# Up tiles with high and low tokens as one 512-column operand, in two mixture-of-neurons layers on one core

## What is computed

```python
sv, si = lax.top_k(sc, PEER_TOPK)
cand = (sv[:, :, 0, :, None] + sv[:, :, 1, None, :]).reshape(c, PEER_HEADS, -1)
best, pos = lax.top_k(cand, PEER_TOPK)
eidx = jnp.take_along_axis(cidx, pos, axis=-1)
g = jax.nn.softmax(best, axis=-1)
a = jnp.einsum('cd,chkd->chk', xc, w_up[eidx]).astype(jnp.float32)
act = (jax.nn.gelu(a, approximate=False) * g).astype(xc.dtype)
return jnp.einsum('chk,chkd->cd', act, w_down[eidx])
```

## Time and profile before

| | |
|---|---|
| median of three runs | 2362.91 us |
| profiled execution, its own time | 2365.95 us |
| its span, first to last instruction | 2363.9 us |
| mean granted TensorE clock | 0.995 |
| up stage of layer 0 | 193.9 to 611.0 us |
| up stage of layer 1 | 1115.1 to 1532.0 us |

### The profile page before, as it was taken

The page is one execution under the profiler, slowest core; times in us unless marked ns, Lnnn a source line. Parts: engine busy times, 40 slices in busy tenths (PEclk is TensorE's granted clock), DMA queues, the critical chain, the costliest instruction groups (busy, mean ns, idle before and its releaser), DMA issues.

```text
span 2363.9 us, 45061 instructions
## 1 busy us (share of the span) xinstructions
PE 2327.5 (98%) x15648; PEld 2089.7 (88%) x15648; DVE 1690.3 (72%) x3195; ACT 1326.6 (56%) x2502; POOL 42.9 (2%) x85
## 2 busy tenths in 40 slices
PE   8999999999999999999999999999999998999998
PEld 8889999999888888899999999988888886788776
DVE  5767996999655555675997799956556577767555
ACT  5655545877545544445455677754555454665454
POOL 1000000000000000000000000000000000000000
PEclk9999999999999999999999999999999999999999
DMA  7455665444566666555556544566665653246454
GB/s 241 129 170 163 183 179 178 137 142 144 179 194 191 192 194 194 163 178 174 183 179 182 157 143 143 161 195 193 208 189 178 182 172 107 72 137 195 129 157 141
DMA packets 137305, 397.44 MB, mean 168 GB/s; under 512 B 12448, under 2 KB 13776, under 8 KB 136400
## 3 DMA queue, kind: packets, MB, share of 16 engines
q1 hardware_dynamic: 134432, 384.97, 54.0%
q0 software_dynamic: 2448, 10.56, 1.3%
q10 hardware_dynamic: 288, 0.10, 0.0%
HBM read 394.54 MB, written 1.05 MB: 167 GB/s over the span
## 4 chain that ended last, share of the span: by engine, by line
PE 91%; DVE 5%; issue 2%; ACT 2%; DMA 0%; DVEq 0%; ACTq 0%; POOLq 0%; POOL 0%; SPq 0%
PE bank L998 31%; PE bank L1014 29%; PE bank L896 12%; PE bank L902 8%; PE bank L1027 4%; PE bank L955 1%; PE bank L943 1%; ACT wh L1336 1%; DVE wl L1731 1%; PE bank L928 1%; PE bank L948 1%; PE bank L979 1%; DVE aux L1769 0%; PE bank L907 0%; PE bank L1212 0%
## 5 line engine op out<-in xcount | busy, mean ns | idle before, releaser
L1731 DVE TENSOR_TENSOR wl<-raw,wh 128x1024 fp32r<-128x1024 f32 (+1 forms) x732 | 893.7, 1222 | 542.9 <-ACT wh L1336 531.7
L1336 ACT ACTIVATE wh<-raw 128x1024 fp32r<-128x1024 f32 (+1 forms) x732 | 771.8, 1055 | 643.5 <-PE bank L1014 337.3
L998 PE MATMUL bank<-xh,wh 128*128 128x256 f32 x2048 | 511.7, 288 | 0.0
L998 PE MATMUL bank<-xl,wh 128*128 128x256 f32 x2048 | 501.9, 283 | 0.0
L998 PEld LDWEIGHTS bank<-xl,wh 128*128 128x128 f32 x2048 | 392.9, 192 | 0.0
L998 PEld LDWEIGHTS bank<-xh,wh 128*128 128x128 f32 x2048 | 392.2, 191 | 0.5
L998 PE MATMUL bank<-xh,wl 128*128 128x256 f32 x2048 | 287.7, 283 | 0.0
L1014 PE MATMUL bank<-wh,gl 128*128 128x512 f32 x1008 | 270.1, 390 | 1.7 <-DVE gl L2113 1.7
L1014 PE MATMUL bank<-wh,gh 128*128 128x512 f32 x1008 | 269.8, 389 | 0.5 <-ACT gh L1510 0.5
L1014 PE MATMUL bank<-wl,gh 128*128 128x512 f32 x1008 | 269.4, 389 | 0.0
L998 PEld LDWEIGHTS bank<-xh,wl 128*128 128x128 f32 x2048 | 264.0, 192 | 1.0 <-DVE wl L1731 0.5
(11 more groups left out here) (300 smaller groups left out, 2675.6 us busy)
## 6 DMA issues: line engine op xcount, KB each, us to landing
raw<-in_w_upT SPq DMA_DIRECT2D x256, 512.0 KB, 3.6
raw<-in_w_down SPq DMA_DIRECT2D x256, 512.0 KB, 4.3
raw<-in_l_w_in SPq DMA_DIRECT2D x84, 512.0 KB, 3.6
raw<-in_peer_w_query SPq DMA_DIRECT2D x32, 512.0 KB, 3.9
raw<-in_l_w_out SPq DMA_DIRECT2D x28, 512.0 KB, 3.7
raw<-in_attn_w_qkv SPq DMA_DIRECT2D x24, 512.0 KB, 4.4
raw<-in_conv_w_in SPq DMA_DIRECT2D x24, 512.0 KB, 3.7
arena<-in_na_bias POOLq DMA_DIRECT2D x4, 1024.0 KB, 7.2
```

Source lines behind the costliest of these rows:

```text
L998: last = pe.matmul(banks[b][:, 0:SEQ], lhsT=w[part][:, k, :], rhs=x_in[xp][:, k, :], start=(k == 0 and part == 0 and xp == 0), stop=(k == ...
L1336: act.activation(wh[:, n % SPLIT, 0:kts * cols], raw[:, n % RAW, 0:kts * cols], ACT.Copy)\
L1731: tt(wl[:, n % SPLIT, 0:kts * cols], raw[:, n % RAW, 0:kts * cols], wh[:, n % SPLIT, 0:kts * cols].bitcast(F32), ALU.subtract).then_inc(lo ...
```

## The change

The high and low tokens become one buffer, `x_both`, of which `xh` and `xl` are halves. For 126 of 128 tiles (`TOGETHER`) the high weights are multiplied with both in one matmul of 512 columns, which fills a whole bank: the high tokens' sum in one half and the low tokens' in the other. The matmuls with the low weights add to the first half. The two halves must then be added. ScalarE copies the bank to a new SBUF buffer `halves`, which frees the bank; GpSimd adds the halves, into `acts` in the first part and into `late` in the second; ScalarE then applies the GELU in place, for two tiles in one instruction in the first part, for one tile in the second. There is one `halves` buffer, which lies where `gl` lies later, so each copy waits for the sum before it.

The first keys' weighing moves from ScalarE (four scaled copies for each quad) to GpSimd (one product of 128x512 with a repeated weight). The second part starts at tile 68 instead of 72, and the 64 quads are spread over 58 tiles instead of 54. The last two tiles keep the old form.

```diff
-FIRST, SLOTS = 72, 54
+FIRST, SLOTS = 68, 58
+TOGETHER = N_KEYS - 2
-        xh, xl = place("xh", [P, KT, SEQ], F32R), place("xl", [P, KT, SEQ], F32R)
+        x_both = place("x_both", [P, 2, KT, SEQ], F32R)
+        xh, xl = x_both[:, 0], x_both[:, 1]
+        halves = place("halves", [P, 2, SEQ], F32, at + 4 * SPLIT * SEQ)
...
GpSimd
+                def weigh_first(q):
+                    pool.wait_ge(onehots, q0 + q + 1)
+                    if q >= FIRSTS:
+                        pool.wait_ge(products, q0 + q - FIRSTS + 1)
+                    c0 = q * QUAD
+                    pool.tensor_tensor(first[:, q % FIRSTS, 0], onehot[:, q % RING, :, 0, :],
+                                       weight_high[:, c0:c0 + QUAD].unsqueeze(2).to_broadcast([P, QUAD, N_KEYS]), ALU.mult)\
+                        .then_inc(first_weighted, 1)
+                with pool.Fori(0, FIRST // 4) as i:
+                    for t in range(4):
+                        pool.wait_ge(up_copied, unit_wait(TOGETHER * layer + t + 1, i))
+                        pool.tensor_tensor(acts[:, bass.ds(i * 4 + t, 1), :].rearrange("p a b -> p (a b)"), halves[:, 0], halves[:, 1], ALU.add)\
+                            .then_inc(up_summed, 1)
+                for q in quads_in(0):
+                    weigh_first(q)
+                for t in range(FIRST, N_KEYS):
+                    for q in quads_in(t - FIRST + 1):
+                        weigh_first(q)
+                    if t < TOGETHER:
+                        pool.wait_ge(up_copied, TOGETHER * layer + t + 1)
+                        if t >= FIRST + 3:
+                            pool.wait_ge(late_weighted, late0 + t - FIRST - 2)
+                        pool.tensor_tensor(late[:, t % 2], halves[:, 0], halves[:, 1], ALU.add).then_inc(up_summed, 1)
...
TensorE, in up
-                        pe.wait_ge(gelu_done, unit_wait(N_KEYS * layer + t - 1, i))
+                        pe.wait_ge(up_copied, unit_wait(TOGETHER * layer + t - 1, i))
+                    if t < TOGETHER:
+                        pe.wait_ge(hi_ready, unit_wait(n + 1, i))
+                        for k in range(KT):
+                            pe.matmul(banks[b].rearrange("p (a b) -> p a b", a=2), lhsT=w[0][:, k, :], rhs=x_both[:, :, k, :],
+                                      start=k == 0, stop=False, skip_group_check=True)
+                        pe.wait_ge(lo_ready, unit_wait(n + 1, i))
+                        for k in range(KT):
+                            last = pe.matmul(banks[b][:, 0:SEQ], lhsT=w[1][:, k, :], rhs=xh[:, k, :], start=False, stop=k == KT - 1,
+                                             skip_group_check=True)
+                        last.then_inc(units_used, 1)
+                        return
...
ScalarE
-                def gelu(t, i=0):
+                def copy_halves(t, i=0):
                     act.wait_ge(units_used, unit_wait(u0 + t + 1, i))
+                    if t or not isinstance(i, int):
+                        act.wait_ge(up_summed, unit_wait(TOGETHER * layer + t, i))
+                    act.activation(halves[:].rearrange("p a b -> p (a b)"), banks[t % 2][:, :], ACT.Copy).then_inc(up_copied, 1)
+                def gelu_pair(t, i=0):
+                    act.wait_ge(up_summed, unit_wait(TOGETHER * layer + t + 2, i))
+                    dst = acts[:, bass.ds(i * 4 + t, 2), :].rearrange("p a b -> p (a b)")
+                    act.activation(dst, dst, ACT.Gelu).then_inc(gelu_done, 2)
+                def two(t, i=0):
+                    for k in (t, t + 1):
+                        copy_halves(k, i)
+                        high(u0 + k + SPLIT, i)
...
+                        for t in (t0, t0 + 2):
+                            gelu_pair(t - 2, i)
+                            two(t, i)
...
                 for k in range(N_KEYS - FIRST):
+                    if FIRST + k < TOGETHER:
+                        copy_halves(FIRST + k)
+                        high(u0 + FIRST + k + SPLIT)
+                        for q in quads_in(k):
+                            hold(q)
+                        late_gelu(FIRST + k)
+                        continue
```

More of the change, by code:

```diff
@@ L507, in build @@
         gelu_done = sem("gelu_done")
+        up_copied, up_summed = sem("up_halves_copied"), sem("up_halves_summed")
         g_high, g_low = sem("gated_high"), sem("gated_low")
@@ L759, in _ @@
                 pool.dma_start(lanes[:], d["c_lanes"].partition_broadcast(P)).then_inc(extra_loaded["lanes"], 16)
+                q0, late0 = QUADS * layer, (N_KEYS - FIRST - 1) * layer
+                def weigh_first(q):
[21 more added lines that the diff above has]
+                        pool.tensor_tensor(late[:, t % 2], halves[:, 0], halves[:, 1], ALU.add).then_inc(up_summed, 1)
                 dump(done)
@@ L1440, in peer @@
                 assert issued[0] == u0 + SPLIT
-                def gelu(t, i=0):
+                def copy_halves(t, i=0):
                     act.wait_ge(units_used, unit_wait(u0 + t + 1, i))
-                    dst = acts[:, bass.ds(i * 4 + t, 1), :].rearrange("p a b -> p (a b)")
-                    act.activation(dst, banks[t % 2][:, 0:SEQ], ACT.Gelu).then_inc(gelu_done, 1)
-                def tiles(t0, t1):
[L1449 to L1456, removed]
+                    if t or not isinstance(i, int):
[9 more added lines that the diff above has]
+                        high(u0 + k + SPLIT, i)
+                def tiles(t0, t1):
+                    if (t1 - t0) % 4:
+                        gelu_pair(t0 - 2)
+                        two(t0)
+                        t0 += 2
+                    with act.Fori(0, (t1 - t0) // 4) as i:
+                        for t in (t0, t0 + 2):
+                            gelu_pair(t - 2, i)
+                            two(t, i)
                 def exponent(t):
@@ L1462, in exponent @@
                     act.activation(g, g, ACT.Exp).then_inc(top_exp, 1)
-                at = 0
+                two(0)
+                gelu_pair(0)
+                two(2)
+                at = 4
                 for t in range(TT):
-                    tiles(at, EXP_TILES[t])
+                    e = EXP_TILES[t]
+                    tiles(at, e)
                     exponent(t)
-                    high(u0 + EXP_TILES[t] + SPLIT)
-                    gelu(EXP_TILES[t])
-                    at = EXP_TILES[t] + 1
+                    two(e)
+                    gelu_pair(e - 2)
+                    two(e + 2)
+                    gelu_pair(e)
+                    at = e + 4
                 tiles(at, FIRST)
+                gelu_pair(FIRST - 2)
                 q0, late0 = QUADS * layer, (N_KEYS - FIRST - 1) * layer
@@ L1476, in late_gelu @@
                     n = QUAD * quads_before(t)
-                    act.wait_ge(units_used, u0 + t + 1)
-                    if t >= FIRST + 3:
+                    if t < TOGETHER:
+                        act.wait_ge(up_summed, TOGETHER * layer + t + 1)
+                        src = late[:, t % 2]
+                    else:
+                        act.wait_ge(units_used, u0 + t + 1)
                         act.wait_ge(late_weighted, late0 + t - FIRST - 2)
+                        src = banks[t % 2]
                     if n:
-                        ins = act.activation(late[:, t % 2, 0:n], banks[t % 2][:, 0:n], ACT.Gelu)
+                        ins = act.activation(late[:, t % 2, 0:n], src[:, 0:n], ACT.Gelu)
                     if n < SEQ:
-                        ins = act.activation(acts[:, t, n:SEQ], banks[t % 2][:, n:SEQ], ACT.Gelu)
+                        ins = act.activation(acts[:, t, n:SEQ], src[:, n:SEQ], ACT.Gelu)
                     ins.then_inc(gelu_done, 1)
[L1486 to L1495, removed]
                 def hold(q):
@@ L1510, in gated_high @@
                     act.activation(gh[:, t % SPLIT, :], src, ACT.Copy).then_inc(g_high, 1)
-                for q in quads_in(0):
-                    weigh_first(q)
                 for k in range(N_KEYS - FIRST):
+                    if FIRST + k < TOGETHER:
[5 more added lines that the diff above has]
+                        continue
                     late_gelu(FIRST + k)
@@ L1518, in peer @@
                         gated_high(0)
-                    for q in quads_in(k + 1):
-                        weigh_first(q)
                     high(u0 + FIRST + k + SPLIT)
-                    for q in quads_in(k):
-                        hold(q)
                 gated_high(1)
```

## The result

The changed kernel takes 2491.3 us (median of four runs, 2490.0 to 2495.1) against 2363.5 us: 1.0543 of the time before, 95% interval 1.0525 to 1.0561. The profiled execution of after has a span of 2488.2 us, 124.3 us longer.

The account below looks back on a forecast made before the run. TensorE bounds the kernel before; beside the router VectorE, held by GpSimd, becomes the bound. Per layer +72 us there and -3 us in the first part; 2363 + 137 = 2500 us, range 2385 to 2600.

Parts of the forecast that it names:

- What bounds: Kernel before: TensorE, busy 98% of the span, sets the pace, with VectorE right behind it beside the router.
- TensorE's part: Up tiles: eight 512-column matmuls replace 16 of 256, saving 0.118 us a tile, 14.9 us a layer.
- Rival 1: Beside the router: VectorE is not excluded, TensorE stays the bound and the kernel takes 2333 us; chance 11%.
- ScalarE's part: Up stage: a 512-column copy takes about 0.59 us; beside the router ScalarE ends lower than its 160 us.
- The exclusion, both directions: GpSimd instructions reading SBUF and VectorE instructions with two SBUF inputs block each other, whichever comes second waiting.
- The price: Time each GpSimd operation holds VectorE: 0.49 us for a sum, 1.02 us for a weighing.
- The router stretch: Tiles 68 to 127: VectorE's 196.7 us plus 93.7 us held by GpSimd make 290 us, +71.8 us a layer.
- The first part: First 68 up tiles: TensorE saves 8.0 us, sums beside the picking of choices give 5 us back, net -3 us.
- The total: Whole kernel: +69 us a layer, 137 us added to the median of 2363 us, giving 2500 us.

Follow-up runs that it names:

- short_ops: Changed kernel with every GpSimd sum and weighing cut to two columns, waits kept, numbers wrong: 2350.6 us, 0.9941 of the kernel before.
- m1_ports: Separate kernel, VectorE and GpSimd running twelve instructions each per phase, alone and together: VectorE's subtractions 13.71 us alone, 19.73 us beside GpSimd's sums.
- long_writes: short_ops plus GpSimd clears of an unused buffer, which read nothing, behind each two-column operation: 2353.0 us, 0.9955 of the kernel before.
- sums_only: Changed kernel with the first keys' weighing back on ScalarE, sums of the halves still on GpSimd: 2363.0 us, 0.9995 of the kernel before.

## Why the prediction was right, and where its steps were not

The forecast was 2500 us, within 2385 to 2600, and the time is 2491. (Its chances for that range add up to 69 + 8 = 77%, not 79.) By its steps:

- **What bounds.** TensorE before, VectorE right behind it beside the router: right. The chain of after passes to VectorE exactly there.
- **TensorE's part, 0.118 us a tile.** Too high. The wide tile steps at 2.79 us, a saving of 0.107 us; beside the router a tile with one quad goes from 3.61 to 3.53 us, 0.08. With everything else out of the way (short_ops) the stage takes 408.7 us instead of 417.1: 8.4 us a layer, not 14.9. Rival 1 should have been priced at 2350, not 2333 us.
- **ScalarE's part.** Right: 0.598 us a copy. It waits 35.8 us for sums beside the router of a layer, and the list of TensorE's waits there doesn't name it.
- **The exclusion, both directions.** Right, and it carries the result: shown by m1_ports (second direction), by long_writes (the waits alone cost nothing), and by VectorE's groups in after.
- **The price.** A sum 0.49 us, measured 0.53. A weighing 1.02 us, measured 0.84: this is the term that was mis-sized. I had let GpSimd take as long as VectorE for twice the elements. For the sum that was near (0.69, measured 0.68 alone), for the weighing not (1.22, measured 1.00), and 0.15 us and not 0.20 of each hold nobody. With the measured figures, 58 x 0.53 + 64 x 0.84 = 84.5 us instead of 93.7. The groups of after agree: 28 us on the subtractions is 0.48 us for each of 58 sums, 53 us on the products 0.83 us for each of 64 weighings.
- **The router stretch.** Forecast 290 us; 196.7 + 84.5 = 281 by the measured prices; measured 280.8. VectorE is busy 277.2 of it, so some 4 us of the holds found cover, and as much idle time came on top. Where it arises isn't shown; at the entry three weighings and a sum follow each other in GpSimd's queue. That next to nothing was covered, as the sum assumed, holds because the weighing is there: in sums_only half of a sum's hold is.
- **The first part.** Forecast -3 us, measured +1.1. Saved are 68 x 0.107 = 7.3 us, given back 8.4 and not 5. Short_ops, with no sums that hold, took 193.0 us where 68 x 2.793 + 0.7 = 190.6: 2.4 us go because VectorE, busy 13.6 of 14 us where it picks, is late without any sum too, once tiles are shorter. The other 5.8 us, up to the 198.8 of after, are the sums'.
- **The total.** A layer came out 10 us below the forecast in the router stretch and 4 us above it in the first part. Between the two profiled executions that makes +124 us where +137 was forecast, and the medians lie 128 us apart. The errors partly cancelled, which is luck; that a held VectorE makes the kernel slower by about this much was the mechanism.

The weighing on GpSimd decides the loss: +75 us alone, and with it the sums no longer fit beneath TensorE's time, another +53. Without it (sums_only) nothing is lost.

The Trainium skill's rule (SBUF — State Buffer, Who interferes with whom), that the second of the two blocks until the first is done, agrees with m1_ports in who excludes whom and who doesn't (reads with two-input instructions; not clears, bank inputs or searches). That the first holds the other for its whole instruction is not quite what was measured: 0.53 of 0.68 us and 0.84 of 1.00 us. Its figure for GpSimd (GPSIMD Engine Reference, Performance versus the Vector engine), taken in proportion as an estimate of 0.56 and 1.12 us, misses the durations alone by 0.12 us each (0.68 and 1.00) and lies above both holds.

## What to carry to other kernels

Before work is moved to an idle engine, ask what it shares with the busy one: here GpSimd had 98% of its time free, and each of its instructions cost VectorE 0.5 to 0.8 us, because one that reads SBUF and one of VectorE's with two SBUF inputs exclude each other. Small operations in the profile of before can show such a lock long before a large one is tried; look for one operation whose time doubles or quintuples beside certain neighbours. And where such work must be placed, put it beside the other engine's reads of PSUM or its one-input searches, and not behind the event that also starts a two-input instruction.

## What the runs showed of the hardware that was not expected

A GpSimd instruction holds VectorE for some 0.15 us less than it takes alone, the same for a sum (0.53 of 0.68 us) and a weighing (0.84 of 1.00 us). A blocked VectorE instruction is shown as longer (0.42 to 1.25 us for a product in m1_ports), with no wait in front of it, so the lists of waits don't show the lock at all. And a GpSimd sum that waits can end up beside a VectorE instruction that reads a bank: in sums_only, with nothing else in its queue, it cost VectorE 0.24 us instead of 0.53, though nobody had placed it there.
